# FFN up GEMMs: the high weights multiply high and low h in one 512-column matmul

## The reference

```python
u = h @ w_up                                  # (256, 2048) @ (2048, 2 * 5632)
up = jnp.pad(u, ((0, 0), (CONV_WIDTH - 1, 0), (0, 0)))
u = sum(conv_w[j] * up[:, j:j + S] for j in range(CONV_WIDTH)) + conv_b   # width 3, per channel
val, gate = jnp.split(u, 2, axis=-1)
return (jax.nn.silu(gate) * val) @ w_down     # (256, 5632) @ (5632, 2048)
```

## Time and profile before

| | |
|---|---|
| median of three executions | 2526.79 us (2526.13 to 2531.17) |
| span of the profiled execution | 2525.9 us, first to last instruction |
| PE busy | 2484.3 us, 98% of the span |
| DVE, ACT, POOL busy | 1440.5, 1124.3, 1232.5 us |
| mean granted TensorE clock | 0.995 of full |

### The profile page before, as it was taken

One profiled execution on the slowest core, in us unless ns is written; L12 is line 12 of the kernel. 1 busy time (PEld: TensorE's weight loads), 2 busy tenths in 40 slices (PEclk: granted clock), 3 DMA queues, 4 the chain that ended last, 5 costly groups with the idle time before them and its releaser, 6 DMA issues.

```text
span 2525.9 us, 50139 instructions
## 1 busy us (share of the span) xinstructions
PE 2484.3 (98%) x19624; PEld 2273.1 (90%) x19624; DVE 1440.5 (57%) x2436; ACT 1124.3 (45%) x1324; POOL 1232.5 (49%) x500
## 2 busy tenths in 40 slices
PE   7999999999999999999999999999999999999997
PEld 5897998899999999998887877899999999998886
DVE  2536666266767767776665633265766756453433
ACT  2253334434444444454444444344544444454443
POOL 2674445675444444454443666465444444444442
PEclk8999999999999999999999999999999999999998
DMA  9974565596777777777776565386666675556553
GB/s 399 397 271 178 200 234 201 224 385 221 276 286 265 267 274 281 267 260 275 272 272 243 182 258 207 130 313 254 220 233 222 216 258 184 184 180 200 192 191 117
DMA packets 140381, 611.66 MB, mean 242 GB/s; under 512 B 15584, under 2 KB 15968, under 8 KB 115680
## 3 DMA queue, kind: packets, MB, share of 16 engines
q1 hardware_dynamic: 140256, 609.88, 66.4%
HBM read 607.72 MB, written 2.10 MB: 241 GB/s over the span
## 4 chain that ended last, share of the span: by engine, by line
issue 45%; PE 33%; POOL 21%; POOLq 1%; DVE 0%; DMA 0%; ACT 0%; DVEq 0%; SPq 0%
PE psum L1971 33%; POOL wlo L1780 21%; POOLq L1777 0%; DMA ada_raw<-adastream 0%; DVE xT L2314 0%; POOLq L1779 0%; PE psum L2204 0%; DVE psum L2314 0%; ACT arena L1794 0%; POOLq L1780 0%; ACT arena L1791 0%; DVE arena L2429 0%; DVE acc L2306 0%; DVE acc L2314 0%; DVEq L388 0%
## 5 line engine op out<-in xcount | busy, mean ns | idle before, releaser
L1780 POOL TENSOR_TENSOR wlo<-raw,whi 128x1024 fp32r<-128x1024 f32 x496 | 1232.3, 2491 | 1264.2 <-ACT whi L1791 1263.2
L1791 ACT ACTIVATE whi<-raw 128x1024 fp32r<-128x1024 f32 x760 | 800.6, 1058 | 950.1 <-PE psum L1971 716.2
L1971 PE MATMUL psum<-hi_h,whi 128*128 128x256 f32 x4224 | 1206.4, 286 | 4.6 <-DVE lo_h L2314 2.3
L1971 PE MATMUL psum<-lo_h,whi 128*128 128x256 f32 x4224 | 1190.3, 282 | 0.0
L1971 PE MATMUL psum<-hi_h,wlo 128*128 128x256 f32 x4224 | 1190.2, 282 | 0.0
L1971 PEld LDWEIGHTS psum<-hi_h,whi 128*128 128x128 f32 x4224 | 798.4, 189 | 18.7 <-issue 8.5
L1971 PEld LDWEIGHTS psum<-hi_h,wlo 128*128 128x128 f32 x4224 | 798.8, 189 | 1.7 <-issue 1.4
L1971 PEld LDWEIGHTS psum<-lo_h,whi 128*128 128x128 f32 x4224 | 798.4, 189 | 0.0
L2306 DVE TENSOR_TENSOR wlo<-raw,whi 128x1024 fp32r<-128x1024 f32 x264 | 385.1, 1463 | 268.3 <-ACT whi L1791 268.3
L2314 DVE SCALAR_TENSOR_TENSOR psum<-ada_raw,cact,psum 128x256 f32<-128x256 f32 x814 | 342.4, 483 | 24.5 <-DMA ada_raw<-adastream 21.1
L1971 PE MATMUL psum<-whi,gshi 128*128 128x512 f32 x704 | 276.0, 392 | 0.3 <-DVE wlo L2306 0.3
(11 more groups left out here) (166 smaller groups left out, 1608.8 us busy)
## 6 DMA issues: line engine op xcount, KB each, us to landing
raw<-wstream SPq DMA_DIRECT2D x760, 512.0 KB, 4.6
ada_raw<-adastream SPq DMA_DIRECT2D x168, 1024.0 KB, 6.8
arena<-adastream SPq DMA_DIRECT2D x24, 1024.0 KB, 18.0
xT<-x_in SPq DMA_DIRECT2D x8, 512.0 KB, 7.1
y_out<-xT SPq DMA_DIRECT2D x4, 512.0 KB, 2.6
gs_pages<-tabs_in SPq DMA_DIRECT2D x2, 512.0 KB, 4.2
gs_pages<-rw_in SPq DMA_DIRECT2D x2, 512.0 KB, 6.7
tabs<-tabs_in SPq DMA_DIRECT2D x1, 482.0 KB, 8.5
```

The source lines that it names most:

```text
L1780: nc.gpsimd.tensor_tensor(wlo[:, q, :], raw[:, q, :], whi[:, q, :].bitcast(F32), ALU.subtract).then_inc(sem.lo_ready, 1)
L1791: return nc.scalar.activation(out_, in_, ACT.Copy, scale=scale)
L1971: return nc.tensor.matmul(o, lhsT, rhs, start=start, stop=stop, skip_group_check=True)
```

## The change

In the tile of h, high and low now stand side by side for each row block: `mx[:, kt, :, :]` is 512 columns, high then low. In the up GEMMs a wide product is two matmuls instead of three: low weights by high h, 256 columns, into the first half of a bank, and high weights by both, 512 columns, into the whole bank. The bank's second half then holds high weights by low h alone, and has to be added at the end. All four tiles j of half 0 are wide (banks 0 to 3) and two of the four of half 1 (banks 4 and 5; the other two stay as they were, in bank 6). At the end of each half ACT copies the second halves out of PSUM into arena (128x1024 in half 0, 128x512 in half 1), DVE adds them to the first halves in PSUM (`sem.low_taken`, `sem.whole`), and then come the taps as before, from other places. ACT's `hi` of slab 11 or 19 now stands between its copy and its taps. DVE's wait and addition stand ahead of `quarter_unit(1, 1)`.

```diff
+WIDE = (4, 2)
-        hi_h, _ = sb("hi_h", [P, KT * S + 128], F32R)
-        lo_h, _ = sb("lo_h", [P, KT * S + 128], F32R)
+        h_parts, _ = sb("h_parts", [P, 2 * KT * S + 128], F32R)
+        hx, mx = (h_parts[:, a:a + 2 * KT * S].rearrange("p (k c s) -> p k c s", c=2, s=S) for a in (0, 32))
...
+        def up_place(half, j):
+            if half == 0 or j < 2:
+                return bank[4 * half + j][:, 0:S]
+            return bank[6][:, (j - 2) * S:(j - 1) * S]
+        def up_sums(half, low):
+            b = 4 * half
+            return psum[:, b:b + WIDE[half], low * S:(low + 1) * S]
... ACT, end of a half
-                        u = pair(1 - half)
+                        copy(tiles(11 + half)[:, 0:WIDE[half], :], up_sums(half, 1)).then_inc(sem.low_taken, 1)
+                        if i is None:
+                            his(z, z + 1)
+                        else:
+                            hi(z, more, i)
+                        act.wait_ge(sem.whole, 2 * (gb + t + step) + half + 1)
                         for j in range(4):
                             c = 16 * half + 4 * j
-                            ins = fn(tiles(11 + half)[:, j, :], u[:, j, :], ACT.Identity,
+                            ins = fn(tiles(11 + half)[:, j, :], up_place(half, j), ACT.Identity,
... PE
+            def slab_up(n, half, k, per=0, i=0):
+                ready(n, per, i)
+                q = n % RING
+                first, last = k == 0, k == GS - 1
+                for kk in range(2):
+                    kt = 2 * k + kk
+                    for j in range(4):
+                        w = slice(kk * 512 + j * P, kk * 512 + (j + 1) * P)
+                        if j < WIDE[half]:
+                            b = bank[4 * half + j]
+                            mm(b[:, 0:S], wlo[:, q, w], mhi[:, kt, :], first and kk == 0, False)
+                            ins = mm(b, whi[:, q, w], mx[:, kt, :, :].rearrange("p c s -> p (c s)"), False, last and kk == 1)
+                        else:
+                            ins = product(up_place(half, j), whi[:, q, w], wlo[:, q, w], mhi[:, kt, :], mlo[:, kt, :],
+                                          first and kk == 0 and j % 2 == 0, last and kk == 1)
...
-                            pe.wait_ge(*st["free"][p])
+                            for p in range(2):
+                                pe.wait_ge(*st["free"][p])
...
-                        pe.wait_ge((sem.free_gate, sem.free_val)[p], NFF * (b + 1))
+                        pe.wait_ge(sem.free_val, NFF * (b + 1))
... DVE, end of a half
                             lo2(lo_at + 6, 2 * GS, i)
+                            dve.wait_ge(sem.low_taken, 2 * (NFF * b + done + i) + half + 1)
+                            tt(up_sums(half, 0), up_sums(half, 0), tiles(11 + half)[:, 0:WIDE[half], :],
+                               ALU.add).then_inc(*at.up(sem.whole))
                             quarter_unit(1, 1)
```

More of the change, by code:

```diff
@@ L245, in __init__ @@
         self.sums_taken = new("sums_taken")
+        self.whole = new("whole")
         self.psum_zero = new("psum_zero")
@@ L258, in __init__ @@
         self.cols_landed = new("cols_landed")
-        self.conv_landed = new("conv_landed")
         self.cw_ready = new("cw_ready")
@@ L268, in __init__ @@
         self.f_abs = new("f_abs")
-        self.f_exp = new("f_exp")
         self.f_ln = new("f_ln")
@@ L282, in __init__ @@
         self.gn_sd = new("gn_sd")
-        self.gn_var = new("gn_var")
         self.gs_hi = new("gs_hi")
@@ L305, in __init__ @@
         self.l2v = new("l2v")
+        self.low_taken = new("low_taken")
         self.lo2_ready = new("lo2_ready")
@@ L406, in build @@
         wlo, _ = sb("wlo", [P, RING, SLAB], F32R)
-        hi_h, _ = sb("hi_h", [P, KT * S + 128], F32R)
-        lo_h, _ = sb("lo_h", [P, KT * S + 128], F32R)
-        hhi, mhi = (hi_h[:, a:a + KT * S].rearrange("p (k s) -> p k s", s=S) for a in (0, 32))
-        hlo, mlo = (lo_h[:, a:a + KT * S].rearrange("p (k s) -> p k s", s=S) for a in (0, 32))
+        h_parts, _ = sb("h_parts", [P, 2 * KT * S + 128], F32R)
+        hx, mx = (h_parts[:, a:a + 2 * KT * S].rearrange("p (k c s) -> p k c s", c=2, s=S) for a in (0, 32))
+        hhi, mhi = hx[:, :, 0, :], mx[:, :, 0, :]
+        hlo, mlo = hx[:, :, 1, :], mx[:, :, 1, :]
         gshi, gs_at = sb("gshi", [P, 2, 4, S], F32R)
@@ L759, in pe_mix1 @@
                 if b:
-                    ins.then_inc(sem.gn_var, 1)
+                    ins.then_inc(sem.gn_mean, 1)
             pe.wait_ge(sem.kept, 3)
@@ L1131, in dve_mix1 @@
             stt(page(15), flat(2), -1.0 / 64, page(15), ALU.mult, ALU.add).then_inc(*at.up(sem.yc))
-            dve.wait_ge(sem.gn_var, 1)
+            dve.wait_ge(sem.gn_mean, 2)
             ts(page(4), flat(2), 1.0 / 64, 64e-5, ALU.mult, ALU.add).then_inc(*at.up(sem.gn_ms))
@@ L1445, in act_mix2 @@
             act.wait_ge(sem.f_abs, 1)
-            fn(f_abs, f_abs, ACT.Exp).then_inc(sem.f_exp, 1)
-            act.wait_ge(sem.f_exp, 1)
+            fn(f_abs, f_abs, ACT.Exp).then_inc(sem.f_ln, 1)
+            act.wait_ge(sem.f_ln, 1)
             fn(f_abs, f_abs, ACT.Ln, bias=1.0).then_inc(sem.f_ln, 1)
@@ L1523, in dve_mix2 @@
             stt(f_abs, f_min, 2.0, gate_in[FORGET], ALU.mult, ALU.subtract).then_inc(*at.up(sem.f_abs))
-            dve.wait_ge(sem.f_ln, 1)
+            dve.wait_ge(sem.f_ln, 2)
             tt(f_min, f_min, f_abs, ALU.subtract).then_inc(*at.up(sem.gt_ready))
@@ L1733, in _ @@
             st["unit"] = START_UNITS
-            sp.dma_start(conv[:], conv_in).then_inc(sem.conv_landed, 16)
+            sp.dma_start(conv[:], conv_in).then_inc(sem.cols_landed, 16)
             for dst, name in ((page(19), "retdecay"), (page(20)[:, 0:S], "alibi")):
@@ L1870, in turn @@
                     for half in range(2):
-                        a, z = n1 + half * GS + 3 + (half == 0), n1 + half * GS + 3 + GS
+                        a, z = n1 + half * GS + 4, n1 + half * GS + 3 + GS
                         if i is None:
@@ L1889, in turn @@
                                 ins.then_inc(sem.gate_tap if half else sem.val_tap, 1)
[L1890 to L1893, removed]
                     act.wait_ge(sem.free_gate, gb + 1 + t + step)
@@ L1991, in slab @@
                                       first and kk == 0 and j % 2 == 0, last and kk == 1)
+                        if kk == 1 and j == 3:
+                            ins.then_inc(sem.slab_used, 1)
+            def slab_up(n, half, k, per=0, i=0):
[13 more added lines that the diff above has]
+                                          first and kk == 0 and j % 2 == 0, last and kk == 1)
                         if kk == 1 and j == 3:
@@ L2155, in body @@
                     for half in range(2):
-                        p = 1 - half
                         free = (sem.free_val, sem.free_gate)[half]
                         if i is None and t == 0:
-                            pe.wait_ge(*st["free"][p])
+                            for p in range(2):
+                                pe.wait_ge(*st["free"][p])
                         else:
@@ L2166, in body @@
                                 pe.wait_ge(sem.h_ready, h0 + k + 1)
-                            slab(n0 + 2 * GS * t + half * GS + k, p, mhi[:, 2 * k:2 * k + 2, :],
-                                 mlo[:, 2 * k:2 * k + 2, :], k == 0, k == GS - 1, 2 * GS * per, 0 if i is None else i)
+                            slab_up(n0 + 2 * GS * t + half * GS + k, half, k, 2 * GS * per, 0 if i is None else i)
                         if units == 2:
@@ L2519, in ffn @@
                 done = 0
+                dve.wait_ge(sem.cols_landed, 32)
                 for turns, units, own in segments:
@@ L2524, in ffn @@
                                                 sem.g_made: 1, sem.acc_ready: units, sem.ada_used: units,
-                                                sem.step: own}) as i:
+                                                sem.whole: 2, sem.step: own}) as i:
                         n1 = n0 + 2 * GS * done
@@ L2556, in ffn @@
                             lo2(lo_at + 6, 2 * GS, i)
+                            dve.wait_ge(sem.low_taken, 2 * (NFF * b + done + i) + half + 1)
+                            tt(up_sums(half, 0), up_sums(half, 0), tiles(11 + half)[:, 0:WIDE[half], :],
+                               ALU.add).then_inc(*at.up(sem.whole))
                             quarter_unit(1, 1)
                             dve.wait_ge((sem.val_tap, sem.gate_tap)[half], NFF * b + done + 1 + i)
-                            u, t = pair(1 - half), tiles(11 + half)
+                            t = tiles(11 + half)
                             marks = []
@@ L2563, in ffn @@
                                 c = 16 * half + 4 * j
-                                stt(t[:, j, 1:S], u[:, j, 0:S - 1], cw[:, c + 1:c + 2],
+                                stt(t[:, j, 1:S], up_place(half, j)[:, 0:S - 1], cw[:, c + 1:c + 2],
```

(2 more changed lines are left out.)

## The result

| | before | after |
|---|---|---|
| median | 2528.09 us | 2673.69 us |
| span of the profiled execution | 2525.9 us | 2670.0 us |
| mean granted TensorE clock | 0.995 | 0.973 |

The account below looks back on a forecast made before the run. The prediction took PE (TensorE), busy 98% of the span, as the bound. Its terms gave 2526.8 - 28.7 + 96 + 22 + 20 = 2636 us, in a range of 2592 to 2675 us.

Parts of the forecast that it names:

- the lagging case: Block 1: finish lags a unit, so PE doesn't stop; only late slabs in both blocks, 2542 us; chance 0.05.
- stops in block 1: Up GEMM of block 1: PE stands 4.85 us after half 0, 3.9 after half 1, 96 us over 11 turns.
- wide matmuls: Up GEMMs of both blocks: 13.6 ns saved on each of 2112 wide products, 28.7 us in all.
- late weights, block 2: Up GEMM of block 2: PE waits for late weights, some 6 us after half 0 and 16 after half 1, together 22.
- clock, block 1: Block 1: stops drop the clock, dense work at half speed costs 1.2 us more each; 20 us in all, bounds 0 and 53.
- 672 in 150 us, 223.2 ns each: Down GEMM: spacing of 512-column matmuls read from a stretch, taken as the wide matmul's cost.
- a sign of being wrong: Up GEMMs: the prediction is wrong if a product's pair of matmuls is not near 342 ns.
- I take three in four: Block 1: share of the 22 stops at which the clock was taken to fall, 20 us.
- dense work of 2.4 us at half speed: After a stop in block 1: the work run at half clock before full speed returns, costing 1.2 us more.
- The place near the start: Start of the kernel: PE stood 2.91 us, the clock fell to half; dense matmuls from 38.54, clock back at 40.9.
- The upper bound of 53 us: Block 1: rival that the clock stays down through much of each half once dropped, 2669 us; chance 0.09.
- the two rivals taken alone (2665 and 2669): Up GEMMs: a wide product saves nothing, 2665 us, chance 0.07; block 1's clock stays down longer, 2669 us, chance 0.09.

Follow-up runs that it names:

- finish_later: The changed kernel with TensorE's finish in block 1 moved two slabs into the next half, VectorE's order kept: 2549.29 us, ratio 1.0082 to the kernel before.
- merge_first: The changed kernel with VectorE's last piece of a unit and its merge moved ahead of the wait for the copy and the addition: 2550.56 us, ratio 1.0092.
- wide_alone: The changed kernel without the copy, the addition and their waits, so high weights by low h is missing from the wide products' sums: 2515.66 us, ratio 0.9951.
- merge_mid: The kernel before, no wide matmul, with VectorE's last piece and merge moved behind a wait for the half's last slab: 2618.54 us, ratio 1.0359.
- early_low: merge_first, with VectorE making the low weights of slabs 11 and 19 right behind the addition, not behind the taps: 2547.95 us, ratio 1.0076.
- both_early: early_low, with ScalarE making the high weights of slab 20 ahead of its wait for Silu, not in the next turn: 2524.76 us, ratio 0.9989.

## Why the prediction was right, and which terms were off

The mechanism held as told: the unit's merge behind the addition, the same unit's `finish` at the end of the same half, 22 stops. finish_later and merge_first show it from both sides, and the lagging case is out. The sizes of two terms did not hold, and the time came out 37 us above the forecast. By the stages, its terms against what was measured:

| term | forecast | measured | by |
|---|---|---|---|
| stops in block 1 | 96 | 90.4 | 4.63 and 3.59 us, 11 times |
| wide matmuls | -28.7 | -11.7 | wide_alone |
| late weights, block 2 | 22 | 13.7 | 512.9 - 499.2 |
| clock, block 1 | 20 | about 53 | 648.5 - 507.0 - (90.4 - 1.8) |
| sum | 109 | 145 | 143.5 by the stages, which leave out the 1.8 us |

(The 1.8 us are the stop in the first turn, 1.6 of them idle, that wide_alone has as well, and before too.)

**The stops.** Right within 6%. After a half 0 PE was to stand for 4.85 us and stood for 4.63. With T = 691.62, where ACT's copy begins, `finish` began at T + 4.36 and not T + 4.45, and PE's last matmul was over at T - 0.27 and not T - 0.40.

**The wide matmul, mis-sized by a factor of 2.4.** The step that failed is "672 in 150 us, 223.2 ns each". The count of a stretch takes in all of PE's instructions, and 16 of those 672 are short transposes (L2204, 128 columns) at the turn of the down GEMM's halves. The same trace has the spacing pure:

```profile
2502.91 0.39 PE L1971 MATMUL psum<-whi,gshi 128*128 128x512 f32 x1
2503.14 0.39 PE L1971 MATMUL psum<-whi,gslo 128*128 128x512 f32 x1
2503.36 0.39 PE L1971 MATMUL psum<-wlo,gshi 128*128 128x512 f32 x1
2503.59 0.39 PE L1971 MATMUL psum<-whi,gshi 128*128 128x512 f32 x1
```

That is 0.68 us for three, 227 ns, and by it the gain would have been 355.2 - 118.4 - 227 = 9.8 ns a product, 21 us. Measured were 5.5 ns, so a 512-column matmul with h moving costs 355.2 - 5.5 - 118.4 = 231 ns, if the narrow one beside it costs what it did. The pair takes 350 ns and not 342, which the prediction had named as a sign of being wrong. A fixed part of 11.7 ns a matmul was the wrong picture: beyond its columns a matmul costs 11.7 ns at 256 of them and some 18 at 512. What makes it so stays open. The Trainium skill ("TensorE: Matmul & The Clock Gate", Part 1, "Wait — 56ns, not 53.3ns?") gives 2.5 ns as the fixed part; as a price of the matmul that goes, the measured 5.5 ns lie nearer to it than to mine, though its spacing at 256 or 512 columns isn't what these traces show.

**The clock, mis-sized by 2.6.** Two steps failed. "I take three in four" was too few: it fell 22 times in 22. And "dense work of 2.4 us at half speed" was too short: 5.8 us of work ran at half speed after the one stop shown and 3.4 after the other, which loses about 2.9 and 1.7 us, where 1.2 were taken. The place near the start from which it was read had thin work ahead of the dense; whether that made it shorter is not shown. The upper bound of 53 us, a rival with a chance of 0.09, is where it came out. What was right is that a stop costs more than itself; what the Trainium skill says of it ("HAM oscillation — how this bites in real kernels", on the same page), a fall at every gap and a price paid each time, is what the trace shows.

**Block 2.** The places were right: weights for slabs 20 and 21 after half 1, and 11 after half 0. The price was 1.2 us a turn instead of 2.0. PE's own waits for `wlo` there are 6.1 us in all; the waits of its weight loads, which come ahead of the matmuls, have the whole 13.8:

```profile
PEld psum L1982 <- DVE wlo L2335: 8.4, 17, 0.7
PEld psum L1982 <- POOL wlo L1790: 5.4, 10, 0.6
```

**The range.** It held by 1.3 us, and that is partly luck. The gain was too large by 17 us and the clock's loss too small by 33, both toward a longer time; only the 14 us too much for waits kept the sum under 2675. The top lies just above each of the two rivals taken alone (2665 and 2669), and here more than half of the one came true and all of the other.

## What to carry to other kernels

Before a wait goes into an engine's order, list what stands behind it and who waits for that, down to the small things: here a merge of 0.42 us, with no part in the change, held up the engine that bounds the kernel. Price a stop of TensorE above its own length: at 22 stops of 2.4 us each lost some 1.6 us more to the clock, at 22 of 3.6 to 4.6 us some 2.4 more. And take the spacing of a form of matmul from a timeline that holds that form alone; a change that saves instructions but no columns was worth 0.5% here, and only once the order around it was free of waits. Where DVE and POOL both subtract, look at which of the two begins first: 0.1 us there moved `acc` by enough to make PE wait 1 us a turn.

## What the runs showed of the hardware that was not expected

- A stop of 2.4 us is enough to lower the clock nearly every time: it fell after 21 of 22 in merge_mid, and only when dense work had already begun again (0.92, then 0.50 in the stretches from 688). Of shorter stops, with a wait of 1.6 us for `acc`, some were followed by a fall and some not: both in merge_first and the one in cw_early were, those in wide_alone, early_low and both_early were not. The waits of 0.5 to 1.0 us for `acc` in these kernels had none behind them.
- The same DVE copy of 32 elements a partition takes 0.17 to 0.23 us or 1.7 to 2.4 us. In block 1 of the kernel before, ten of the eleven begin while POOL's subtraction runs, and each ends 0.03 to 0.05 us after POOL's (the first of them from 666.95 for 1.86 us, POOL from 666.28 for 2.49); the eleventh meets none of POOL's and takes 0.17.
- The two engines keep each other out in either order: begun just after POOL's, DVE's subtraction took 3.35 us instead of 1.23; begun just after DVE's, POOL's took 3.46 instead of 2.40. That shows who waited and how long, not what the two share.
